# Two transformer blocks in one kernel: the experts' input half with exponentials a head later, eight row buffers, low parts an octet later, and first output parts made in its tail

## The reference, cut to what matters

```
q = (xi @ w_q).reshape(n, 8, 2, 128)
s = einsum('nhpc,hpkc->nhpk', q, sub_keys)          # 2 x 128 key scores per token and head
ts, ti = top_k(s, 16)
cand_s = ts[:, :, 0, :, None] + ts[:, :, 1, None, :]  # 16 x 16 candidates
best_s, best_p = top_k(cand_s, 16)
idx  = the 16 chosen experts of 128 * 128, per token and head
gate = softmax(best_s)
act  = gelu(einsum('nd,nhkd->nhk', xi, u[idx]))
out  = einsum('nhk,nhkd->nd', gate * act, v[idx])
```

## Time and profile before

| | before |
|---|---|
| median of three runs | 2726.69 us |
| the profiled execution | 2725.89 us |
| its span | 2724.2 us |
| PE busy | 2427.8 us (89%) |
| DVE busy | 1794.6 us (66%) |
| ACT busy | 1059.3 us (39%) |
| POOL busy | 644.7 us (24%) |
| mean granted PE clock | 0.938 of full |

### The profile page before, as it was taken

How to read it: one execution, slowest core, us unless ns; L and a number is a source line. 1 busy time by engine, 2 the same in 40 slices (tenths; PEclk the granted TensorE clock), 3 DMA queues, 4 the chain that set the end, 5 groups by cost and what they waited for, 6 DMA issues and landing times.

```text
span 2724.2 us, 36788 instructions
## 1 busy us (share of the span) xinstructions
PE 2427.8 (89%) x12966; PEld 1336.6 (49%) x12966; DVE 1794.6 (66%) x2961; ACT 1059.3 (39%) x1495; POOL 644.7 (24%) x482
## 2 busy tenths in 40 slices
PE   7996668998888876877879999999899999999998
PEld 3344344554445544555545555556445444444444
DVE  5228675568788885667578888885735345777335
ACT  4255222555555543333333333333342223333224
POOL 0003241366667763111042222220400000000001
PEclk9996778999999988999989999999999999999999
DMA  4200002376777765666799999993333332333221
GB/s 159 78 8 0 1 1 70 126 231 220 234 237 237 236 236 183 251 217 229 259 361 382 375 366 370 372 365 108 101 101 105 103 99 81 108 100 101 94 92 55
DMA packets 169938, 480.02 MB, mean 176 GB/s; under 512 B 17728, under 2 KB 75968, under 8 KB 168928
## 3 DMA queue, kind: packets, MB, share of 16 engines
q1 hardware_dynamic: 113664, 293.92, 31.7%
q0 software_dynamic: 36864, 134.23, 13.9%
q10 hardware_dynamic: 19296, 50.34, 4.9%
HBM read 426.00 MB, written 52.43 MB: 176 GB/s over the span
## 4 chain that ended last, share of the span: by engine, by line
PE 68%; DVE 17%; ACT 4%; DMA 4%; POOL 3%; issue 3%; DVEq 1%; SPq 0%; ACTq 0%; POOLq 0%
PE psum L496 20%; PE psum L497 20%; PE psum L498 20%; DVE arena L1876 3%; DMA arena<-in_urows,arena 3%; POOL arena L476 2%; DVE arena L470 1%; PE psum L987 1%; PE psum L386 1%; DVEq L1803 1%; PE psum L988 1%; DVE arena L618 1%; ACT arena L457 1%; POOL arena L2142 1%; PE psum L807 1%
## 5 line engine op out<-in xcount | busy, mean ns | idle before, releaser
L496 PE MATMUL psum<-arena 128*128 128x384 f16 (+3 forms) x3648 | 1273.5, 350 | 106.9 <-ACT arena L1375 59.9
L497 PE MATMUL psum<-arena 128*128 128x384 f16 (+3 forms) x3648 | 1275.6, 350 | 0.0
L498 PE MATMUL psum<-arena 128*128 128x384 f16 (+3 forms) x3648 | 1267.6, 349 | 0.0
L496 PEld LDWEIGHTS psum<-arena 128*128 128x128 f16 (+1 forms) x3648 | 357.5, 98 | 444.8 <-issue 68.4
L470 DVE SCALAR_TENSOR_TENSOR arena<-arena 128x1024 f16<-128x1024 f32 x216 | 268.8, 1245 | 404.2 <-ACT arena L457 403.7
L498 PEld LDWEIGHTS psum<-arena 128*128 128x128 f16 (+1 forms) x3648 | 356.4, 98 | 329.7 <-issue 16.6
L497 PEld LDWEIGHTS psum<-arena 128*128 128x128 f16 (+1 forms) x3648 | 356.7, 98 | 317.1 <-issue 15.4
L457 ACT ACTIVATE arena<-arena 128x1024 f16<-128x1024 f32 x216 | 226.6, 1051 | 284.0 <-PE psum L498 268.0
L476 POOL TENSOR_TENSOR arena<-arena 128x1024 f16<-128x1024 f32 x104 | 222.1, 2136 | 164.2 <-ACT arena L465 161.8
L1876 DVE CUSTOM_DVE_ANT_0 arena<-arena 128x1024 f32<-128x1024 f32 x128 | 206.3, 1638 | 81.7 <-DMA arena<-in_urows,arena 80.8
L1442 ACT ACTIVATE arena<-arena 128x1024 f16<-128x1024 f32 x128 | 135.2, 1057 | 298.5 <-PE psum L498 298.0
(11 more groups left out here) (250 smaller groups left out, 2250.4 us busy)
## 6 DMA issues: line engine op xcount, KB each, us to landing
arena<-in_w SPq DMA_DIRECT2D x320, 512.0 KB
arena<-in_v SPq DMA_DIRECT2D x128, 512.0 KB
early_activations<-arena ACTq DMA_DIRECT2D x128, 192.0 KB
gate_matrix<-arena ACTq DMA_DIRECT2D x6, 4096.0 KB, 13.6
arena<-gate_matrix SPq DMA_DIRECT2D x32, 768.0 KB
arena<-early_activations SPq DMA_DIRECT2D x128, 192.0 KB
arena<-in_xT SPq DMA_DIRECT2D x4, 512.0 KB, 6.4
arena<-in_urows,arena POOLq DMA_INDIRECT x128
```

The lines of the kernel that those rows point to most:

```text
L496: nc.tensor.matmul(ps, a_h, b_h, start=first, stop=False)
L497: nc.tensor.matmul(ps, a_h, b_l, start=False, stop=False)
L498: return nc.tensor.matmul(ps, a_l, b_h, start=False, stop=last)
```

## The change

- `gate_exp(h)` is no longer called in turn 7 of head h but in turn 1 of head h+1 (the last one in the gap, at e = 81).
- The ring of fetched rows has 8 buffers for the picks below 92 and from 128 on, and 4 between (`row_use`). The four added buffers (`more_rows`) lie where the second `G` buffer lies in the tile turns. LEAD is 12.
- In the tile turns VectorE makes in octet i the low part that it made in octet i-1.
- SyncE loads the first four slabs of `v` before slabs 172 to 175, and slabs 176 to 179 after the gates and activations of group 0.
- In the tail VectorE makes the coefficients, 12 own additions and three low parts of `v` between the low parts of the slabs; ScalarE makes the high parts of group 0 there, and the high part of the first gated product before the last gelu.
- Some pairs of semaphores are merged into one (`wz_cut`, `lam_step`, `p_cut`), with the same waits.

```diff
-ROWS = 4
+ROWS = 8
+ROWS_G = 4
-LEAD = 8
+LEAD = 12
+HEAD_PICKS = (PH - 1) * TURN_PICKS + GAP_PICKS
+def row_use(k):
+    if k < HEAD_PICKS:
+        return k % ROWS, k // ROWS
+    if k < PICKS:
+        return k % ROWS_G, (HEAD_PICKS + ROWS_G) // ROWS + (k - HEAD_PICKS) // ROWS_G
+    b = (k - PICKS) % ROWS
+    first = row_use(PICKS - ROWS_G + b)[1] + 1 if b < ROWS_G else HEAD_PICKS // ROWS
+    return b, first + (k - PICKS) // ROWS
...
@@ sync @@
-            slabs(N_PQ + SLOTS, N_POOL + SLOTS)
+            slabs(N_PQ + SLOTS, N_U + TAIL_AT // SLOTS * SLOTS + 2 * SLOTS)
             sp.wait_ge(g_done, GT * OCT * 2)
             for s in range(GRP):
                 sp.dma_start(vraw[:, s, :], io["v"][s]).then_inc(vslab_in[s], 16)
+            slabs(N_U + TAIL_AT // SLOTS * SLOTS + 2 * SLOTS, N_POOL)
             for s in g_stored:
                 sp.wait_ge(s, GT // 2 * 16)
...
             load_group(0, 0, first=True)
+            slabs(N_POOL, N_POOL + SLOTS)
             load_group(1, 1)
@@ scalar @@
-                    if j == WEAVE - 3:
-                        gate_exp(h)
+                    if j == 1 and h:
+                        gate_exp(h - 1)
...
             for e in range(WOVEN, WOVEN + GAP):
                 spilled(e)
+                if e == WOVEN + 1:
+                    gate_exp(PH - 1)
...
+            for e in range(TAIL_AT, NK):
+                cuts.upto(N_U + e + 3)
+                if e == NK - 1:
+                    gated_high(0, 0)
+                spilled(e)
+                if e == TAIL_AT:
+                    act.wait_ge(own_dotted, PICKS)
+                    nc.scalar.activation(own_coef, own_dot, ACT.Gelu).then_inc(own_acted, 1)
+                if e == NK - GRP - 1:
+                    act.wait_ge(g_stored[0], GT // 2 * 16)
+                if NK - GRP - 1 <= e < NK - 1:
+                    value_high(0, e - (NK - GRP - 1))
+            store_early(NK - 1, (NK - 1) % 4)
+            for s in range(1, GRP):
+                if s == GRP - 1:
+                    value_high(1, 0)
+                gated_high(0, s)
@@ vector @@
                     one_hots(t * OCT + i)
-                    if t == 0 and i == 0:
+                    if t == 0 and i == 1:
                         dve.wait_ge(low_cut, cuts.n)
-                    cuts.upto(N_U + e + (i + i // 4 + (i % 4 == 3)) // 2 + 3)
+                    if i:
+                        cuts.upto(N_U + e + (i - 1 + (i - 1) // 4 + ((i - 1) % 4 == 3)) // 2 + 3)
+                    elif t:
+                        cuts.upto(N_U + e - 1 + 3)
...
+            for e in range(TAIL_AT, NK):
+                i = e - TAIL_AT
+                cuts.upto(N_U + e + 3)
+                if i == 1:
+                    dve.wait_ge(own_acted, 3)
+                    dchain.link(nc.vector.scalar_tensor_tensor(out=own_coef, in0=own_coef, scalar=WS, in1=own_gate,
+                                                               op0=ALU.mult, op1=ALU.mult))
+                if i in (2, 3):
+                    for pick in range(2 * i - 4, 2 * i - 2):
+                        own_add(pick, pick, 0)
+                if e >= NK - GRP:
+                    for pick in range(2 * (e - NK + GRP) + 4, 2 * (e - NK + GRP) + 6):
+                        own_add(pick, pick % ROWS, pick // ROWS)
+                if e >= NK - 3:
+                    value_low(0, e - (NK - 3))
+            for s in range(GRP):
+                if s == GRP - 1:
+                    value_low(0, s)
+                gated(0, 0, s)
+                own_add(s + LEAD, (s + LEAD) % ROWS, (s + LEAD) // ROWS)
+                gated_low(0, s)
@@ gpsimd, own_fetch @@
+                b = row_use(k)[0]
+                if k >= PICKS + ROWS:
+                    pool.wait_ge(own_added, k - PICKS - ROWS + 1)
+                elif k >= PICKS + ROWS_G:
+                    if k == PICKS + ROWS_G:
+                        pool.wait_ge(g_stored[1], GT // 2 * 16)
+                elif k >= HEAD_PICKS:
+                    pool.wait_ge(own_dotted, k - ROWS_G + 1)
+                elif k >= ROWS:
+                    pool.wait_ge(own_dotted, k - ROWS + 1)
```

More of the change, by code:

```diff
@@ L92 @@
 TILE_PICKS = 6
-LEAD = 8
-assert (PH - 1) * TURN_PICKS + GAP_PICKS + GT * TILE_PICKS == PICKS
+LEAD = 12
[8 more added lines that the diff above has]
+    return b, first + (k - PICKS) // ROWS
+assert HEAD_PICKS + GT * TILE_PICKS == PICKS and HEAD_PICKS % ROWS == ROWS_G and PICKS % ROWS == 0
 def build(nc, io, out):
@@ L244, in build @@
         gsum = r.take(16)
+        assert r.at >= region_g + P * NT
+        more_rows = v3(r.take((ROWS - ROWS_G) * D), ROWS - ROWS_G)
+        assert r.at <= region_g + 2 * P * NT
         assert r.at <= WORDS
@@ L281, in build, with own_row @@
         ptmp = v3(r.take(2 * T), 2)
+        def own_row(b):
+            return own_rows[:, b, :] if b < ROWS_G else more_rows[:, b - ROWS_G, :]
         consts_in, vecs_in, ones_in, meta_in = sem("consts_in"), sem("vecs_in"), sem("ones_in"), sem("meta_in")
@@ L698, in _ @@
                 n1.sum(pe, c)
-            pe.wait_ge(lam_prod, 1)
-            nc.tensor.matmul(bank(2, 2), ones[0:DH, :], LAMP[0:DH, :], start=True, stop=True).then_inc(lam_sum, 1)
+            pe.wait_ge(lam_step, 1)
+            nc.tensor.matmul(bank(2, 2), ones[0:DH, :], LAMP[0:DH, :], start=True, stop=True).then_inc(lam_step, 1)
             pe.wait_ge(consts_in, 176)
@@ L1156, in _ @@
                 n6.sum(pe, c)
[L1158 removed]
+            pe.wait_ge(p_cut, 2)
             for c in range(KC):
@@ L1430, in _ @@
                 tile_turn(t)
-            for e in range(TAIL_AT, NK):
-                spilled(e)
-                if e == TAIL_AT + 3:
-                    act.wait_ge(own_dotted, PICKS)
-                    nc.scalar.activation(own_coef, own_dot, ACT.Gelu).then_inc(own_acted, 1)
-            store_early(NK - 1, (NK - 1) % 4)
             def value_high(g, s):
@@ L1930, in _ @@
                 tile_turn(t)
-            for e in range(TAIL_AT, NK):
-                cuts.upto(N_U + e + 3)
             def gated(g, par, s):
@@ L1948, in gated_low, with value_low, value_group @@
                                         ALU.subtract).then_inc(a_cut, 1)
-            def value_group(g, par, own=True):
+            def value_low(g, s):
+                dve.wait_ge(vhigh_cut, g * GRP + (s + 1))
+                nc.vector.scalar_tensor_tensor(out=vl[:, s, :], in0=vraw[:, s, :], scalar=WS, in1=vh[:, s, :],
+                                               op0=ALU.mult, op1=ALU.subtract).then_inc(vlow_cut, 1)
+            def value_group(g, par, turn=None):
                 for s in range(GRP):
-                    dve.wait_ge(vhigh_cut, g * GRP + (s + 1))
-                    nc.vector.scalar_tensor_tensor(out=vl[:, s, :], in0=vraw[:, s, :], scalar=WS, in1=vh[:, s, :],
-                                                   op0=ALU.mult, op1=ALU.subtract).then_inc(vlow_cut, 1)
+                    value_low(g, s)
@@ L1956, in value_group @@
                     gated(g, par, s)
-                    if own:
-                        own_add(g * GRP + (s + LEAD), s, g + LEAD // GRP)
+                    if turn is not None:
+                        own_add(g * GRP + (s + LEAD), (1 - par) * GRP + s, turn)
                     gated_low(g, s)
-            dve.wait_ge(own_acted, 3)
-            dchain.link(nc.vector.scalar_tensor_tensor(out=own_coef, in0=own_coef, scalar=WS, in1=own_gate,
-                                                       op0=ALU.mult, op1=ALU.mult))
@@ L1964, in _ @@
-            for pick in range(LEAD):
-                own_add(pick, pick % ROWS, pick // ROWS)
-            value_group(0, 0)
+            for e in range(TAIL_AT, NK):
[13 more added lines that the diff above has]
+                    value_low(0, e - (NK - 3))
@@ L1971, in _ @@
             dve.wait_ge(own_added, PICKS)
             nc.vector.tensor_tensor(own_sum[0], own_sum[0], own_sum[1], ALU.add).then_inc(own_added, 1)
-            value_group(GROUPS - 2, 0, own=False)
-            value_group(GROUPS - 1, 1, own=False)
+            value_group(GROUPS - 3, 1)
+            value_group(GROUPS - 2, 0)
+            value_group(GROUPS - 1, 1)
             for c in range(KC):
```

65 lines of the change are left out of this document (29 added, 36 removed).

## The result

The changed kernel takes 2628.4 us (median of four runs, 2625.6 to 2631.0), the kernel before, on the same chip, 2726.9 us; the ratio is 0.9644 [0.9632, 0.9655]. Forecast were 2609 us, in a range of 2592 to 2645. Its profiled execution took 2629.15 us, 96.7 less than that of before.

The account below looks back on a forecast made before the run. VectorE was taken to bound the heads, waits among ScalarE, VectorE and TensorE the tile turns, TensorE the output half. 2725.9 - 41 (heads) - 70 (turns) - 6.7 (changeover) = 2608 us profiled, so 2609; range 2592 to 2645.

Parts of the forecast that it names:

- Sum: Whole kernel: 41 us off the heads, 70 off tile turns, 6.7 off the changeover, giving 2608 us profiled, 2609 median.
- rival 2: Heads: a loop through exponentials, fetch and low part sets 58.2 us a head; gain 19, not 41; 2631 us; chance 0.11.
- Tile turns: Tile turns: low parts an octet later remove most waits, 36.0 us a turn, gain 70 us (40 to 76).
- Rivals 1, 3 and 4: Tile turns: half the waits stay, 2639 (0.17); ScalarE equally later, 2679 (0.06); slab loads delayed, 2751 at 40 us (0.04).
- Heads, the cause: Heads: eight buffers free GpSimd's fetches and later exponentials keep ScalarE from stopping it, so 50.0 us of row waits go.
- Heads, the price: Heads: dots slowed by denser GpSimd low parts cost 1 us a head, 6 in all (bounds 0 and 12).
- Heads, head 1: Head 1: late `head_done` of head 0 delays the fourth row's dot, 12.8 us lost, against 10.0 of row waits saved.
- Changeover: Changeover to the output half: TensorE stands 8.5 us instead of 15.18, gain 6.7 us (bounds 10 and -5).
- Signs: Right: choices 54 to 55 us apart, changeover wait 5 to 12 us. Wrong: choices over 57, ScalarE waiting for slabs.

Follow-up runs that it names:

- e3: The changed kernel with the low parts of the tile turns cut in the same octet as their high parts again: 2701.8 us.
- e1: The changed kernel with each head's exponentials back in the seventh turn of their own head, eight row buffers kept: 2657.6 us.
- e2: The changed kernel with four buffers for fetched rows in the heads, as before, the later exponentials kept: 2614.7 us.
- b4: The changed kernel, eight buffers kept, with GpSimd's fetch held until the whole batch of four dots two batches back has ended: 2619.7 us.
- e5: The changed kernel with only head 0's exponential back in the seventh turn of its own head: 2612.3 us.
- e6: The changed kernel with slabs 176 to 178 cut behind the tail, before the last group of the output half: 2622.8 us.
- e7: The changed kernel with slabs 176 to 179 issued before SyncE waits for the stored gated rows: 2623.6 us.
- e4: The changed kernel with the tail of the input half, its loads and the first output parts as before: 2619.6 us.

## Why the prediction was right or wrong, step by step

- *Sum.* Forecast 117.7 us of gain in the profiled execution, measured 96.7: turns 70.0 of 70, heads 33.3 of 41, changeover -5.3 of +6.7, output half -2.4 of 0, 1.3 ahead of the first mark. The time lies inside the range, but nearer to rival 2 (2631) than to the forecast. That is chance: rival 2 had heads worth 19 and a changeover that gains. One sum of the prediction is wrong: its bounds added end to end (30 + 40 - 5) reach to 2661 us and not to 2646.
- *Tile turns.* Right in mechanism and size: stores 35.7 us apart (36.0 forecast), clock 1.00, no loads late. e3 shows that the edit carries it alone. Rivals 1, 3 and 4 are out.
- *Heads, the cause: the step that failed.* "With eight buffers GpSimd can fetch at its own pace ... So the 50.0 us go." They went, but through the other edit: with the buffers alone 58.8 us of row waits stay (e1), without them 29.7, of which 12 before the last choice ends (e2). The prediction had itself called the two waits one loop, and still did not ask what either edit gives alone: the exponentials 45 us, the buffers 4 without them and -12 beside them.
- *Heads, the price.* "If the excess grows in that proportion it is 1 us a head." Over the six heads from choice 1 to choice 7 VectorE's busy time rose from 313.9 to 323.6 us, 9.7 where 6 were forecast with a bound of 12 (2.8 us a head in the first five, less than before in the last). The term is the right size, but not what was meant: the dots, whose excess was to grow, fell from 1.85 to 1.76 us. Other instructions came to lie beside low parts: the cast at L1876 takes 0.23 us before and in e1, 2.17 in the changed kernel and 2.66 in e2, the comparison at L1879 1.22, 1.40, 2.13 and 2.13. So that came with the later exponentials and not with the buffers. The Trainium skill ("SBUF — State Buffer", section "Who interferes with whom") gives as the rule that the two engines exclude each other and that the issue order decides who stands; dots, low parts and the fetch of 1.76 us agree. The casts go further: one that starts inside a fetch stands through the low part behind it as well (last section). The prediction read from the rule that the number of meetings would stay and the term would be near 0. The number changed with both edits: 26 of 60 dots took over 1.3 us before, 18 in the changed kernel, 15 in e2, 11 in b4.
- *Heads, head 1.* 12.8 us were charged for the late `head_done` of head 0 (584.8 forecast, 582.6 measured), less 10.0 of row waits: 2.8 lost up to the end of choice 1, where 7.0 were. e5 puts the price of the late exponential at 16 us by the medians and 20 by the marks. VectorE leads from there to the end, and nothing later absorbs it. Rival 2 is out as a mechanism: choices 2 and 3 end 58.0 and 57.4 us behind the ones before them, near its 58.2, but VectorE is busy 56.8 and 56.1 us of that, so it is work that holds them and no loop. TensorE is busy all the time there too, but with 342 and 344 matmuls where a head has 304: it gains ground. ScalarE waits for the difference only from choice 4 on, 23.0 us in all.
- *Changeover: the other step that failed.* "Slab 176 coming late adds about 3.5." The store landed at T+17.3, as forecast (T+18), the slab was issued at T+20.2 (T+23), but it landed at T+42 and not T+30: its load took 21.8 us where 7 were allowed. Ten fetches of rows, gates, activations and four slabs were asked for within 14 us, and the queues moved 405 GB/s with DMA busy all the time. The lower bound had been tied to a late store, not to this. e6 and e7 show the cause; e4, that the whole tail edit is worth -9.3 us.
- *Signs.* Of the signs of being right, a changeover wait of 5 to 12 us (17.6 measured), choices 54 to 55 us apart and ScalarE's wait near 0 did not come. Two of the signs of being wrong did: choices over 57 us apart, twice, and ScalarE waiting for a weight slab.

## What to carry to other kernels

When two waits form one loop, price the two cures as alternatives and try each alone: here one gave 45 us and the other took 12 of them back. A deeper buffer also changes when its producer works, and a producer that excludes the engine that bounds can cost more than the waits it saves. Where an engine handles operands in a fixed order, look up what each load it meets there has beside it, not what the load takes by itself.

## What the runs showed of the hardware

- A dot on VectorE that starts behind a GpSimd subtraction on 128 x 1024 stands until that has ended: 3.01 us for 1.22 (2.1 where the subtraction has half the size). It hits small instructions too (a cast of 128 x 128 at 2.17 us on average in the changed kernel and 2.66 in e2, for 0.23), while index searches and reductions kept their times (285 ns after and 287 before, 1209 and 1205). The cast in the kernel before, and in the changed one, five heads:

```profile
L1841 DVE CAST arena<-arena 128x128 f32<-128x128 uint32 x5 | 1.1, 228 | 0.4
```

```profile
L1876 DVE CAST arena<-arena 128x128 f32<-128x128 uint32 x5 | 10.8, 2169 | 0.4
```

Four of these five start 0.54 us before a fetch ends, stand through the low part that follows it, and end 0.1 us after that; the fifth meets neither and takes 0.23 us. One of the four, GpSimd first:

```profile
863.10 1.76 POOL L2202 DMA_INDIRECT arena<-in_urows,arena  x1 [0.15 <-issue]
864.88 2.00 POOL L497 TENSOR_TENSOR arena<-arena 128x1024 f16<-128x1024 f32 x1
```

```profile
864.32 2.65 DVE L1876 CAST arena<-arena 128x128 f32<-128x128 uint32 x1
```

- One core moved 405 GB/s for 27 us at the changeover, 373 over 400 us of the output half. A slab of 512 KB then took 21.8 us, and the 4 MB stores of `G` 16.7 us (median) in turns of 35.7 us, against 13.6 in those of 47.8, in e3 as in the kernel before.
